# One delta-rule and state-space step: the first quarter's tables of the state-space stage made in the stage before it, and one room for both stages' activations

## The reference: what is computed

```python
def gdn_chunked(q, k, v, g, beta, s0):        # delta rule: scan over chunks
    def step(s, xs):
        u = u0_c - jnp.einsum('bhcd,bhde->bhce', w_c, s)
        o = jnp.einsum('bhcd,bhde->bhce', qg_c, s) + jnp.einsum('bhij,bhje->bhie', attn_c, u)
        s = gl_c[..., None, None] * s + jnp.einsum('bhcd,bhce->bhde', kd_c, u)
...
def s5_scan(u, x0, lam_re, lam_im, log_dt, b_re, b_im, c_re, c_im, d):
    lam_bar = jnp.exp(lam * dt)
    b_bar = ((lam_bar - 1) / lam)[..., None] * b
    bu = jnp.einsum('blgc,gpc->blgp', uf.astype(jnp.complex64), b_bar)
    # x_t = lam_bar x_{t-1} + bu_t ;  y_t = Re(c x_t) + d u_t
```

## Time and profile before

| | |
|---|---|
| executions shown | 1130.44, 1130.65, 1136.3 us, median 1130.65 |
| profiled execution | 1127.33 us, its span 1125.6 us |
| TensorE busy | 1023.6 us, 91% of the span |
| VectorE busy | 575.9 us, 51% |
| ScalarE busy | 355.0 us, 32% |
| GpSimd busy | 225.3 us, 20% |
| mean granted TensorE clock | 0.944 |

### The profile page before, as it was taken

The page is one execution under the profiler, slowest core; times in us unless marked ns, Lnnn a source line. Parts: engine busy times, 40 slices in busy tenths (PEclk is TensorE's granted clock), DMA queues, the critical chain, the costliest instruction groups (busy, mean ns, idle before and its releaser), DMA issues. The chain is left out here.

```text
span 1125.6 us, 15469 instructions
## 1 busy us (share of the span) xinstructions
PE 1023.6 (91%) x5432; PEld 603.1 (54%) x5432; DVE 575.9 (51%) x1272; ACT 355.0 (32%) x729; POOL 225.3 (20%) x366
## 2 busy tenths in 40 slices
PE   3899999899999889978998989999769999999975
PEld 3466666544587677766887445444433333333332
DVE  3243445777435856568883253547672332332248
ACT  6121221114311364332331443333213333332333
POOL 0100000068341334413111000002142121111060
PEclk9999999999999888897997999999869999999988
DMA  9685525201011510038761920131447977699283
GB/s 333 201 236 190 217 85 214 75 39 76 38 15 29 117 38 1 1 92 280 268 227 30 339 75 20 41 129 38 134 121 254 333 246 253 231 354 366 106 321 132
DMA packets 126930, 177.07 MB, mean 157 GB/s; under 512 B 37406, under 2 KB 81683, under 8 KB 126840
## 3 DMA queue, kind: packets, MB, share of 16 engines
q1 hardware_dynamic: 117510, 147.03, 38.8%
q0 software_dynamic: 6432, 18.96, 5.1%
q10 hardware_dynamic: 2906, 10.02, 2.2%
HBM read 129.06 MB, written 45.85 MB: 155 GB/s over the span
## 5 line engine op out<-in xcount | busy, mean ns | idle before, releaser
L371 PE MATMUL bank<-hw 128*128 128x344 f32 x576 | 169.7, 456 | 3.8 <-ACT hw L555 3.8
L371 PEld LDWEIGHTS bank<-hw 128*128 128x128 f32 x576 | 109.8, 191 | 62.0 <-issue 5.4
L2232 PE MATMUL bank<-hw,H 128*64 (+1 forms) x608 | 135.1, 597 | 2.1 <-ACT hw L2312 2.1
L456 PE MATMUL bank<-hw 128*128 128x512 f32 x256 | 114.7, 605 | 4.3 <-ACT qkvT L583 4.3
L2668 PE MATMUL bank<-hw 128*128 128x512 f32 x232 | 106.5, 602 | 0.5 <-DVE hw L1974 0.5
L2232 PEld LDWEIGHTS bank<-hw,H 128*64 128x64 f32 x608 | 44.0, 138 | 88.9 <-issue 88.9
L456 PEld LDWEIGHTS bank<-hw 128*128 128x128 f32 x256 | 64.2, 254 | 50.5 <-issue 32.1
L2250 PE MATMUL bank<-yy,H 128*64 128x512 f32 (+1 forms) x304 | 71.1, 611 | 2.2 <-ACT H L2291 2.1
L2312 ACT ACTIVATE hw<-hw 128x2048 f32 x19 | 36.3, 1911 | 109.1 <-PE bank L2232 90.2
L2335 DVE COPY H<-bank 128x256 f32<-128x256 f32 x19 | 8.1, 424 | 115.6 <-PE bank L2215 115.6
L2668 PEld LDWEIGHTS bank<-hw 128*128 128x128 f32 x232 | 41.7, 190 | 44.1 <-issue 41.5
(11 more groups left out here) (565 smaller groups left out, 1833.5 us busy)
## 6 DMA issues: line engine op xcount, KB each, us to landing
ys_d<-ZO SPq DMA_DIRECT2D x18, 1024.0 KB, 12.9
yy<-in_w_down SPq DMA_DIRECT2D x16, 1024.0 KB, 10.4
hw<-in_w_gate SPq DMA_DIRECT2D x16, 1024.0 KB, 7.3
hw<-in_w_up SPq DMA_DIRECT2D x16, 1024.0 KB, 10.9
ys_d<-H ACTq DMA_DIRECT2D x19, 512.0 KB, 6.9
hw<-in_w_in SPq DMA_DIRECT2D x4, 2048.0 KB, 8.2
yy<-in_w_ada SPq DMA_DIRECT2D x4, 2048.0 KB, 8.7
hw<-in_w_ada SPq DMA_DIRECT2D x8, 1024.0 KB, 12.2
```

Source lines behind the costliest of these rows:

```text
L371: mm = t.matmul(ps[3 * (m % 2) + s][:, 0:SEG], w_ring[:, q % 2, k, (m % 4) * P:(m % 4 + 1) * P], hT[:, k, s * SEG:(s + 1) * SEG], start=(k ...
L456: mm = t.matmul(ps[b % 4][0:n, :], tok, w_ring[:, q % 2, k, :], start=(k == 0), stop=(k == KD - 1))
L2232: mm = t.matmul(ps[2 + p][lane, :], xT[p][:, k, lane], wgu[:, bass.ds(bufs[j], 1), k, :].rearrange("p o n -> p (o n)"), start=(k == 0), st ...
```

## The change

W and CL of quarter 0 are made by VectorE in the delta rule's main loop: W in chunk 3, in two halves of 4 groups (6 instructions on 128x512), CL's even groups in chunk 4 and odd groups in chunk 5 (3 instructions on 128x576 each). They are placed ahead of `merge1(c + 1)`. Temporaries lie in the room of masks that are no longer read. TensorE turns W behind the last chunk, ahead of the last two `out_transposes`, and ScalarE evicts it to BM and BS between the last two `oT`, after the sample-state DMAs have landed, whose room they take. In the state-space block quarter 0 then begins with the turned inputs, and K comes ahead of the state inputs. So that W and CL can be written while the delta rule runs, ZO and yy become one room: W0 lies at its start, CL0 in the part of Yt that quarter 0 does not write. `tail` moves to the projection's block, and the router's small tensors to the room of Vd.

```diff
+        ZO = msb("ZO", [P, 18, GW])
+        yy = ZO[:, :, :].rearrange("p i n -> p (i n)")[:, 0:4 * T + 9 * GW]
+        Yt = yy[:, 4 * T:4 * T + 9 * GW].rearrange("p (i n) -> p i n", i=9)
+        W0 = yy[:, 0:NG * LAGS * CH].rearrange("p (g k c) -> p g k c", g=NG, c=CH)
+        def CL0(x, first, last):
+            return Yt[:, x // 2, P + (x % 2) * CLN + first * CH:P + (x % 2) * CLN + last * CH]
...
@@ delta rule, SyncE
-                sp.dma_start(O["gdn_p"][0, 0].rearrange("h k v -> k h v"), S).then_inc(s_out, 16)
-                sp.wait_ge(s_out, 16 * (1 + DEC))
+                sp.dma_start(O["gdn_p"][0, 0].rearrange("h k v -> k h v"), S).then_inc(p_out, 16)
+                sp.wait_ge(s_out, 16 * DEC)
+                sp.wait_ge(p_out, 16)
@@ delta rule, TensorE, behind the loop over chunks
+                act.wait(t, f"Z2_{NT - 1}")
+                dve.wait(t, f"Y{NT - 1}")
+                dve.wait(t, "W0")
+                for x in range(NG):
+                    mm = t.transpose(ps[x // 4][:, (x % 4) * P:(x % 4 + 1) * P], W0[:, x].rearrange("p j c -> p (j c)"), ident[:, :])
+                pe.did(mm, "BM0")
                 out_transposes(NT - 2)
                 out_transposes(NT - 1)
@@ delta rule, ScalarE
                 oT(NT - 2)
+                pe.wait(a, "BM0")
+                a.wait_ge(s_out, 16 * DEC)
+                input_tables(a, act, "BM0")
                 oT(NT - 1)
@@ delta rule, VectorE
+                def early(dst, lam, first, n, x, y, name):
+                    shape = [P, 4, n, CH]
+                    tmp = masks[:, 0:4 * n * CH].rearrange("p (g k c) -> p g k c", g=4, c=CH)
+                    dve.drain(v)
+                    dve.did(v.tensor_tensor(dst, lam[0][:, :, first:first + n].unsqueeze(3).to_broadcast(shape), x.unsqueeze(2).to_broadcast(shape), ALU.mult))
+                    dve.did(v.tensor_tensor(tmp, lam[1][:, :, first:first + n].unsqueeze(3).to_broadcast(shape), y.unsqueeze(2).to_broadcast(shape), ALU.mult))
+                    dve.drain(v)
+                    dve.did(v.tensor_tensor(dst, dst, tmp, ALU.add), name)
...
+                    if c == 3:
+                        early_W()
+                    elif c in (4, 5):
+                        if c == 4:
+                            pe.wait(v, "oT2")
+                        early_CL(c - 4)
                     if c + 1 < NT:
                         merge1(c + 1)
@@ state space, TensorE
                 turn_rows(0)
+                turn_decode(0)
                 for q in range(4):
...
-                    dve.wait(t, f"W{q}")
-                    for x in range(NG):
-                        mm = t.transpose(ps[x // 4][:, (x % 4) * P:(x % 4 + 1) * P], W[:, x].rearrange("p j c -> p (j c)"), ident[:, :])
-                    pe.did(mm, f"BM{q}")
-                    if q == 0:
-                        turn_decode(0)
-                        state_inputs(0)
-                    else:
+                    if q > 0:
+                        dve.wait(t, f"W{q}")
+                        for x in range(NG):
+                            mm = t.transpose(ps[x // 4][:, (x % 4) * P:(x % 4 + 1) * P], W[:, x].rearrange("p j c -> p (j c)"), ident[:, :])
+                        pe.did(mm, f"BM{q}")
                         act.wait(t, f"yp{q - 1}")
-                    dve.wait(t, f"CL{q}")
+                        dve.wait(t, f"CL{q}")
                     for x in range(NG):
                         mm = t.matmul(ps[4 + x // 4][0:CH, (x % 4) * P:(x % 4 + 1) * P], Bb[:, gs[x], :],
-                                      CL[:, x, 0:LAGS, :].rearrange("p k c -> p (k c)"), start=True, stop=True)
+                                      outputs_table(q, x, 0, LAGS), start=True, stop=True)
                     pe.did(mm, f"K{q}")
-                    if q > 0:
-                        state_inputs(q)
+                    state_inputs(q)
@@ state space, VectorE, tables(q)
+                    if q > 1:
+                        pe.wait(v, f"BM{q - 1}")
                     if q > 0:
-                        pe.wait(v, f"BM{q - 1}")
-                    table(W[:, :, :, :], Wt[:, :, 0:LAGS, :], LB, Bb[:, gs, :], B2[:, gs, :], LAGS, ALU.add, f"W{q}")
+                        table(W[:, :, :, :], Wt[:, :, 0:LAGS, :], LB, Bb[:, gs, :], B2[:, gs, :], LAGS, ALU.add, f"W{q}")
...
-                    table(CL, Wt[:, :, :, :], LC, q1, q2, LAGS + 1, ALU.add, f"CL{q}")
+                    if q > 0:
+                        table(CL, Wt[:, :, :, :], LC, q1, q2, LAGS + 1, ALU.add, f"CL{q}")
```

More of the change, by code:

```diff
@@ L139, in emit @@
         qkvT = msb("qkvT", [P, MQ, T])
[L140 to L143, removed]
+        masks = msb("masks", [P, 3 * P + 256])
+        upper, neg_lo, big_up = (masks[:, n * P:(n + 1) * P] for n in range(3))
+        pick = masks[:, 3 * P:3 * P + 256].rearrange("p (m n) -> p m n", m=8)
         HB, BL = NT * HEADS, 32
@@ L164, in emit @@
         pre = s2.enter_context(nc.sbuf_tensor("pre", [P, 2, 3 + T], F32))
+        tail = s2.enter_context(nc.sbuf_tensor("tail", [P, MQ, 3 + DEC], F32))
         convd = s2.enter_context(nc.sbuf_tensor("convd", [P, MQ, 3, DEC], F32))
@@ L1058, in kd_t, with input_tables @@
             return hT[:, HEADS:2 * HEADS, c * P:(c + 1) * P]
+        def input_tables(a, act, name):
+            for bnk in range(2):
+                src = ps[bnk][:, :].rearrange("p (g n) -> p g n", g=4)
+                part = slice(4 * bnk, 4 * bnk + 4)
+                act.did(a.activation(BM[:, part, :], src, ACT.Copy))
+                act.did(a.activation(BS[:, part, 0:ST], src[:, :, ST:P], ACT.Copy))
+                act.did(a.activation(BS[:, part, ST:P], src[:, :, 0:ST], ACT.Copy, scale=-1.0), f"{name}_{bnk}")
         with nc.Block() as block:
@@ L1472, in merge2, with early_W, early_CL @@
                     dve.did(v.tensor_copy(Y[0:64, c % 2, :, 64:P], heads(ps[1][0:64, 0:256])), f"Y{c}")
+                def early(dst, lam, first, n, x, y, name):
[6 more added lines that the diff above has]
+                    dve.did(v.tensor_tensor(dst, dst, tmp, ALU.add), name)
+                def early_W():
+                    for half_ in range(2):
+                        gs = slice(4 * half_, 4 * half_ + 4)
+                        early(W0[:, gs], [LB[:, n, gs] for n in range(2)], 0, LAGS, Bb[:, gs, :], B2[:, gs, :], "W0")
+                def early_CL(odd):
+                    gs = slice(odd, NG, 2)
+                    at = P + odd * CLN
+                    q1, q2 = (x[:, 0, :].rearrange("p (g c) -> p g c", c=CH)[:, gs] for x in (Q1, Q2))
+                    early(Yt[:, 0:4, at:at + CLN].rearrange("p t (k c) -> p t k c", c=CH), [LC[:, n, gs] for n in range(2)], 0, LAGS + 1, q1, q2, f"CL0_{odd}")
                 merge1(0)
@@ L1533, in emit @@
         CS2 = t4("CS", [P, 2, NG, LAGS, CH])
-        BM, BS, U, zin, z2, Zc, Zs, TT = (wr[:, :, i * P:(i + 1) * P] for i in range(KD))
+        U, zin, z2, Zc, Zs, TT = (wr[:, :, i * P:(i + 1) * P] for i in range(2, KD))
         TT = TT.rearrange("p g (j c) -> p g j c", j=LAGS)
@@ L1657, in state_inputs @@
                     for x in range(NG):
-                        if x % 4 == 0:
+                        if q > 0 and x % 4 == 0:
                             act.wait(t, f"BM{q}_{x // 4}")
@@ L1744, in _ @@
                     act.did(a.activation(Ud[:, :, :, :].rearrange("p g v b -> p (g v b)"), ps[6][:, P:P + 2 * NG * DEC], ACT.Copy), f"U{q}")
-                    pe.wait(a, f"BM{q}")
                     if q > 0:
+                        pe.wait(a, f"BM{q}")
                         pe.wait(a, f"x1_{q - 1}")
-                    for bnk in range(2):
-                        src = ps[bnk][:, :].rearrange("p (g n) -> p g n", g=4)
-                        part = slice(4 * bnk, 4 * bnk + 4)
-                        act.did(a.activation(BM[:, part, :], src, ACT.Copy))
-                        act.did(a.activation(BS[:, part, 0:ST], src[:, :, ST:P], ACT.Copy))
-                        act.did(a.activation(BS[:, part, ST:P], src[:, :, 0:ST], ACT.Copy, scale=-1.0), f"BM{q}_{bnk}")
+                        input_tables(a, act, f"BM{q}")
                     pe.wait(a, f"K{q}")
@@ L1852, in emit @@
         X2 = sb("X2", [P, 9, D])
-        combine = sb("combine", [P, 9, 2])
-        pos = sb("pos", [P, 9, 2], U32)
-        slot_t = sb("slot_t", [1, MOST + 1, 8], I32)
-        exp_t = sb("exp_t", [1, EXPERTS], I32)
+        late_room = room(Vd_room[:, :])
+        combine, pos = late_room(P, 9, 2), late_room(P, 9, 2).bitcast(U32)
+        slot_t, exp_t = late_room(1, MOST + 1, 8).bitcast(I32), late_room(1, EXPERTS).bitcast(I32)
         w_out = wr
-        b_r = sb("b_r", [P, EXPERTS])
+        b_r = late_room(P, EXPERTS)
         land6, rland = sem("land6"), sem("rland")
```

20 lines of the change are left out of this document (11 added, 9 removed).

## The result

Against the kernel before in the same runs, the changed kernel's ratio is 1.0045 [1.0026, 1.0064] (8 runs of each, medians 1137.87 and 1130.35 us). A second comparison gave 1.0015 [0.9994, 1.0036] (12 runs against 29, medians 1133.68 and 1132.32). By these ratios it costs 2 to 5 us, with ends of the intervals at a gain of 1 and a loss of 7. A loss is likely, and its size is open: the quotient of the first two medians alone is 1.0067. The forecast was a gain of 1.1 us, to 1129.5, and the first median lies outside its range, above 1134.5. The profiled executions are less alike than the medians: before 1127.33 us, near the low end of its runs, after 1141.01 us, at the top of its own.

What follows compares the result with a forecast made beforehand. TensorE was taken as the bound (busy 91%), with waits and half clock in state-space quarter 0. Block -4.3, delta rule's end +0.2, loop +3.0 gave -1.1 us: from 1130.65 to 1129.5, range 1124.5 to 1134.5.

Steps and rivals of the forecast that it cites:

- Gain of the block: 4.3 us: State-space block: quarter 0's output products start 2.6 us earlier and run 1.7 us faster; bounds 1.0 and 6.2.
- Its first term: State-space quarter 0: state inputs complete at +11.0 after the block's start instead of +15.0, 4 us earlier.
- The second ends where the transfer rate falls ... +17.5: State-space quarter 0: second adaLN load lands at +17.5 after the block's start; TensorE waits some 2 us for it.
- the term of 2.6 us: State-space quarter 0: output products start at +23.5 after the block's start instead of +26.1.
- The term of 1.7 us for the clock: Output products of quarter 0: a 4 us stretch at 0.58 clock goes, saving 1.7 us.
- as long as before: Later state-space quarters: stay TensorE bound at unchanged length, all shifted by the same time.
- Loss of the loop: 3.0 us: Delta rule's loop: GpSimd copies held by new VectorE instructions cost 1.4 us in chunk 4, 1.6 in chunk 5.
- The end of the delta rule: After the last chunk: turning W and ScalarE's six evictions cost 0.2 us, up to 2.2.
- The block's gain doesn't come (the weights): State-space block: second adaLN load at +17.5 regardless, half clock after; gain only 1.0, total 1132.9 us; chance 0.10.
- the clock rival: Delta rule chunks 4 and 5: late merge idles TensorE, clock falls; loop loss 8.0 us, total 1134.5; chance 0.15.
- The gaps didn't hold: Delta rule's idle VectorE stretches: rival that copies don't contend, loss only 0.7 us, total 1127.2; chance 0.27.

Runs made afterwards that it cites:

- the two variants: Changed kernel with quarter 0's K after the state inputs (ratio 1.0004); changed kernel with eight small TT transfers held until the second adaLN load landed (1.0022).
- K behind: Changed kernel with K of quarter 0 put after the state inputs again, as before the change: ratio to before 1.0004, 1133.32 us.
- loads first: Changed kernel with the phases of quarter 1 issued after the first two adaLN loads instead of ahead of them: ratio to before 1.0002, 1131.66 us.

## Why the prediction was wrong

**The step that failed: "Gain of the block: 4.3 us".** Its first term held: state inputs complete at +11.9 for +11.0. The second did not: "The second ends where the transfer rate falls ... +17.5". The rate does fall at +17.9, but the load landed at +20.7 (+20.8 and +20.3 in the two variants, +20.6 in the second profile). The prediction took the first load's landing from its own row (L1556, 11.5 us) and the second's from the fall of the rate, without looking at the row of the second (L1559). The row shown above has it: 14.1 us is the longest there. The second of L1559's two issues began at about 509.1, so it landed at 523.2, or +18.5, already 1.0 behind the forecast. Now the longest is 16.5, from an issue at 513.3, which is just where TensorE was released. In the three other kernels with the old block the same sum gives +18.9, +19.7 and +19.8 (if there, too, the longest is the second's). TensorE's wait was 4.8 us, not 2. The second block ran at 3.64, as forecast (3.8), and the turns behind it took 2.9 for 2.2. Output products started at +27.2, for +23.5 forecast and +26.1 before: 3.2 of the 3.7 us are the landing. So the term of 2.6 us was a loss of 1.1. The term of 1.7 us for the clock came in quarter 0 (the 5.7 for 7.3 us of the products), but the later quarters, which I had "as long as before", took 24.4, 26.0 and 24.1 us for 22.8, 23.1 and 25.6 in the first profile. The earlier trace rows is a stretch at full clock, and the last quarter of before already wasn't one. In six profiles with the new block and its loads in their old order it took 110.7 to 114.1 us, mean 112.3. In the four with the old block it took 108.6, 108.8, 111.3 and 113.9, mean 110.7. Values so few and so spread show no sure loss, and a gain of 4.3 does not fit them.

**The loop: "Loss of the loop: 3.0 us".** Right in sum, wrong in its parts, so right by luck. Against the one profile of before, the delta rule lost 4.1 and 1.9 us in the two profiles of after, and 4.1, 2.3, 4.1 and 2.1 in four others with the same loop work. The mean is 3.1, for 3.2 forecast with the block's end. The copies are held by the two-input instructions, as I took it, and as the Trainium skill, page "SBUF — State Buffer", section "Who interferes with whom", has it. The trace agrees with the rule: 2.90 and 2.73 for four copies of 1.33 in all. Chunk 3 cost nothing, as said: TensorE took up the merge's product at 457.76 against 457.70. Chunk 4 cost nothing either, where I had 1.4, because the clock was back sooner; that was not the tables' doing, for in the kernel without them it was back as soon and chunk 4 took 12.8 us. Chunk 5 cost 2.6 and chunk 6 1.8, where I had 1.6 and nothing. No instruction was stretched in chunk 5; this is the half clock. In this profile the mechanism is the rival to which I gave 0.15: an idle TensorE in chunk 4 and a slow chunk 5. It came with 1.21 us of idleness, below the 1.5 or so that I had named. It is not the whole loss, and not always there. In the four profiles with such a chunk 5 (12.8 to 13.2 us) TensorE had been idle for 1.21, 1.20, 1.00 and 0.62 us. In the two others with the same loop (K behind, loads first) it was idle for 0.54 and 0.53, the clock stayed at 1.00 for two stretches more and then lost one (0.59 and 0.60), chunks 4 to 6 took 13.5, 12.0 and 7.8 us, and the loss was still 2.3 and 2.1. And an idle of 0.69 (before, at 474.31) was not followed by a fall, one of 0.70 in the kernel without the tables was. So the tables cost 1.9 to 4.1 us with or without a chunk 5 at half clock; how the loss divides between the late merges and the clock is not separated.

**The end of the delta rule**, 0.2: right. From the last merge to the block's end it is 18.3 us before and 18.3 after.

**The rivals.** "The block's gain doesn't come (the weights)", 0.10, and the clock rival, 0.15, both came true, in one profile; the weights landed later still than that rival's +17.5. I had priced each alone, at 1132.9 and 1134.5, and ended the range at the dearer of the two. Together they give 3.9 + 3.3 = 7.2 us, 1137.9, above it. That was the fault of the range: nothing makes the two exclude one another, since each is a wait of TensorE in its own block that can take the clock with it. That 1137.9 is just the first median is luck, since the second comparison's ratio is 1.0015. The gaps didn't hold: that rival is out.

**Still open.** Why the load lands later than with the old block (+20.0 to +20.9 for +18.5 to +19.8) is not settled. Two comparisons rule out K's transfers and K's place; the place in the queue moves it (+16.0 with the phases behind), but that is a cure and no cause, and its 4.7 us are more than the bytes account for. Nor do I know why the clock falls in one later quarter or in another: the changed kernel's two profiles differ in it with the same program. For the kernel before there is one profile, so what its own loop varies by is not known. The spread of the two ratios, 1.0045 and 1.0015, may come from that.

## What to carry to other kernels

An idle stretch that ends in a wait for another engine is not free room: first ask why that engine is late, because moving its six short copies ahead of one wait brought some 8 us, while filling the stretch brought none and lost most of what the better order gave. Read a transfer's landing from its own column, not from the rate. Where two rivals don't exclude one another, give the range their sum.

## What the runs showed of the hardware

- VectorE with two SBUF inputs holds GpSimd's copies with one input too (1.33 to 2.90), and is held by GpSimd's two-input work: 0.69 to 2.27 beside an instruction of 1.9 us. VectorE with one SBUF input held neither GpSimd's copies nor its mask (1.32 and 1.03 beside a reciprocal of 3.35), nor, at full rate, two copies (0.63 beside 0.67) or its two-input scaling (1.89 beside 0.69).
- A VectorE reciprocal of 128x512 took 3.35 us, a tensor_tensor of that size 0.69.
- A wait of 1.21 us in TensorE was followed by about 12 us at 0.50 to 0.53 of the clock, and the chunk took 13.2 instead of 10.6 us. Waits of 0.62 and 0.70 were followed by a fall to 0.50 as well; after waits of 0.53, 0.54 and 0.69 the next stretch stood at 1.00.
- The second of two 1 MB loads landed 1.0 us behind the fall of the DMA rate in the kernel before and 2.9 us behind it in the changed one.
- Untouched code of 111 us took 108.6 to 113.9 us in four kernels, with TensorE busy for 100.1 to 104.6 us of it.
